# Moving the rows of a modulation product into the first mixer of a two-block transformer kernel

## The reference, cut to what matters

```python
def ada_mod(cond, w, b):
    m = jax.nn.silu(cond) @ w + b          # w: 1024 x 6144
    return jnp.split(m, N_MOD, axis=-1)
sh1, sc1, g1, sh2, sc2, g2 = ada_mod(c, w_ada, b_ada)              # for the tokens: all six used
csh1, csc1, ... = ada_mod(c_ctx, w_ada, b_ada)                     # for the context: two used
hx2 = modulate(rms_norm(x, norm2_g), sh2, sc2)                     # h * (1 + scale) + shift
x = x + g2 * sqrelu_mlp(hx2, w_mlp1, w_mlp2)
```

## Time and profile before

| | |
|---|---|
| median of 3 runs | 2599.49 us (2598.84 to 2599.61) |
| the profiled execution | 2597.69 us, its span 2595.9 us |
| PE busy | 2567.7 us, 99% |
| DVE, ACT, POOL busy | 1739.3 us (67%), 1172.8 us (45%), 206.0 us (8%) |
| DMA moved | 406.14 MB, mean 156 GB/s |
| PE's clock granted | 0.999 of full speed |

### The profile page before, as it was taken

The page is one execution under the profiler, slowest core; times in us unless marked ns, Lnnn a source line. Parts: engine busy times, 40 slices in busy tenths (PEclk is TensorE's granted clock), DMA queues, the critical chain, the costliest instruction groups (busy, mean ns, idle before and its releaser), DMA issues.

```text
span 2595.9 us, 41811 instructions
## 1 busy us (share of the span) xinstructions
PE 2567.7 (99%) x16880; PEld 2148.2 (83%) x16880; DVE 1739.3 (67%) x2471; ACT 1172.8 (45%) x1844; POOL 206.0 (8%) x245
## 2 busy tenths in 40 slices
PE   8999999999999999999999999999999999999999
PEld 7887878787888887887989878977887888888887
DVE  6454454559999978898725564566667777768573
ACT  6454444536444443356432343244545555554331
POOL 2121222300100001132000000000000000000000
PEclk9999999999999999999999999999999999999999
DMA  4101111235777799983423212121543444487763
GB/s 142 42 26 42 35 41 34 73 124 176 253 242 252 266 375 335 336 294 138 159 87 131 67 60 69 42 76 59 197 157 117 154 154 141 158 326 279 242 223 136
DMA packets 290769, 406.14 MB, mean 156 GB/s; under 512 B 15760, under 2 KB 162704, under 8 KB 290576
## 3 DMA queue, kind: packets, MB, share of 16 engines
q1 hardware_dynamic: 276464, 352.07, 39.7%
q0 software_dynamic: 14112, 51.39, 5.8%
HBM read 314.27 MB, written 89.13 MB: 155 GB/s over the span
## 4 chain that ended last, share of the span: by engine, by line
PE 70%; DVE 6%; DMA 3%; issue 2%; ACT 1%; SPq 0%; DVEq 0%; ACTq 0%
PE ps L973 14%; PE ps L903 7%; PE ps L905 7%; PE ps L901 7%; PE ps L579 3%; PE ps L563 3%; PE ps L566 3%; PE ps L689 3%; PE ps L1160 3%; PE ps L693 3%; PE ps L691 3%; PE ps L1161 2%; PE ps L1165 2%; PE ps L1135 1%; DVE mraw L2460 1%
## 5 line engine op out<-in xcount | busy, mean ns | idle before, releaser
L901 PE MATMUL ps<-Bh,Ah 128*128 128x512 f32 x896 | 349.6, 390 | 1.4 <-ACT vb L1715 1.4
L903 PE MATMUL ps<-Bh,Al 128*128 128x512 f32 x896 | 348.8, 389 | 1.5 <-DVE Al L2336 1.5
L2127 DVE TENSOR_TENSOR Wlo<-Wraw,Whi 128x1024 fp32r<-128x1024 f32 x100 | 124.6, 1262 | 217.5 <-ACT Whi L1533 217.4
L905 PE MATMUL ps<-Bl,Ah 128*128 128x512 f32 x640 | 249.0, 389 | 0.0
L1737 ACT ACTIVATE ftr_h<-ftr_r 128x1024 fp32r<-128x1024 f32 x112 | 118.6, 1059 | 237.6 <-DMA ftr_r<-b_scratch 237.4
L973 PE MATMUL ps<-ftr_l,wgt_h 128*128 128x512 f32 x848 | 210.1, 390 | 4.0 <-DVE ftr_l L2404 4.0
L689 PE MATMUL ps<-Whi,Hh 128*128 128x256 f32 x736 | 212.2, 288 | 0.0
L973 PE MATMUL ps<-ftr_h,wgt_h 128*128 128x512 f32 x848 | 210.0, 390 | 0.0
L973 PE MATMUL ps<-ftr_h,wgt_l 128*128 128x512 f32 x848 | 209.6, 389 | 0.0
L693 PE MATMUL ps<-Whi,Hl 128*128 128x256 f32 x736 | 208.2, 283 | 0.0
L691 PE MATMUL ps<-Wlo,Hh 128*128 128x256 f32 x736 | 208.2, 283 | 0.0
(11 more groups left out here) (383 smaller groups left out, 5463.6 us busy)
## 6 DMA issues: line engine op xcount, KB each, us to landing
b_scratch<-qb SPq DMA_DIRECT2D x224, 256.0 KB, 3.0
wgt_r<-in_m_w SPq DMA_DIRECT2D x112, 512.0 KB, 4.8
ftr_r<-b_scratch SPq DMA_DIRECT2D x112, 512.0 KB, 6.1
pair<-in_m_w SPq DMA_DIRECT2D x128, 256.0 KB, 3.2
mraw<-in_w_ada POOLq DMA_DIRECT2D x64, 512.0 KB, 4.6
Wraw<-in_w_in SPq DMA_DIRECT2D x56, 512.0 KB, 4.1
other<-in_m_w SPq DMA_DIRECT2D x32, 512.0 KB, 5.6
mraw<-in_m_w1T POOLq DMA_DIRECT2D x32, 512.0 KB, 5.1
```

What stands on the lines that cost most here:

```text
L901: e.matmul(o, h[:, k, :], Bh[x][:, k, :], start=first and k == 0, stop=False, skip_group_check=not first)
L903: e.matmul(o, l[:, k, :], Bh[x][:, k, :], start=False, stop=False, skip_group_check=not first)
L905: i = e.matmul(o, h[:, k, :], Bl[x][:, k, :], start=False, stop=k == 3, skip_group_check=not first)
L2127: e.tensor_tensor(Wlo[n % 4][:], Wraw[n % 2][:], Whi[n % 4][:].bitcast(F), ALU.subtract).then_inc(*S("w_lo", "v").tick(n))
```

## The change

Units 0 to 48 go into `MIX`: three after steps of head 0's g, six after steps of f for heads 1, 3 and 5, four after steps of q for heads 1 to 5, four after steps of g for heads 2 and 4. Units 49 to 65 go to the MLP's first stage at n = 8, 10, ... 40, the diagonal to n = 42, the shift row to product 44, units 66 to 97 to n = 46, 48, ... 108. The second stage has none left. The buffers of the tokens' rows are now two tiles of `R1` that the mixer has free (6 and 7, the vector in 5); ACT's copy into `R1` at tail 2 of heads 5 to 7 waits for unit 48, and SP's reload of x in the second stage for unit 97.

```diff
+            if (kind == "f" and h in (1, 3, 5) and i in (0, 1, 3, 4, 6, 7) or kind == "q" and 1 <= h < 6 and i in (0, 1, 4, 5)
+                    or kind == "g" and h in (2, 4) and i in (0, 1, 4, 5) or kind == "g" and h == 0 and i in (1, 4, 5)):
+                MIX.append(("mod", u, None))
+                u += 1
...
-        MODS = {}
-        for g in range(4, 53):
-            MODS[g] = [] if 8 <= g < 16 else list(range(49, NU))[sum(map(len, MODS.values())):][:2 if 18 <= g < 26 else 1]
+        DIAG, ROW = 42, 44
+        MODS = {**{8 + 2 * i: 49 + i for i in range(17)}, **{46 + 2 * i: 66 + i for i in range(32)}}
...
+                    if s == ROW and not j:
+                        shift_row()
...
-                            sp.wait_ge(S("ada").at(48))
+                            sp.wait_ge(S("ada").at(NU - 1))
...
+                        if h > 4:
+                            act.wait_ge(S("ada").at(48))
                         e.activation(R1[:, h, :], ps[:], ACT.Copy).then_inc(*freed(("tail", h, 2), 0))
...
+                elif kind == "mod":
+                    modulation(h)
...
+            def row_load(u):
+
+                if u % 49 >= 2:
+                    pool.wait_ge(S("ada").at(u - 2))
+                j = u - 1 if u < 49 else u - 50
+                e.dma_start(mod_place(u), w_ada[j] if u < 66 else m2_w1T[u - 66]).then_inc(*S("ada_raw", u % 2).tick(u, 16))
+
+            pool.wait_ge(sq_of(1).at((1, 7, 1, 0)), H1.lo_at(7))
+            vector_load(0)
...
+                if kind == "mod":
+                    if h < 48:
+                        row_load(h + 1)
```

More of the change, by code:

```diff
@@ L192, in build @@
         other = [at(f"other{i}", [P, 1024], F, WRA + 4096 * i) for i in range(2)]
-        cvec, shr = sa("cvec", 13), sa("shr", 12)
-        mraw = [[at(f"mraw{i}", [P, T], F, R1A + 22528 + 4096 * i) for i in range(2)], [sa("mraw2", 14), sa("mraw3", 15)]]
+        cvec, shr = [R1[:, 5, :], sa("cvec", 13)[:]], sa("shr", 13)
+        mraw = [[R1[:, 6 + i, :] for i in range(2)], [at(f"mraw{i}", [P, T], F, R1A + 22528 + 4096 * i)[:] for i in range(2)]]
         facc = [at(f"facc{a}", [P, T], F, H_(6 + a)) for a in range(2)]
@@ L321, in build @@
         MIX += [*in_turn(more, rest, 1), ("split", 7, None)]
+        mixed, MIX, u = MIX, [], 0
+        for step in mixed:
+            MIX.append(step)
+            kind, h, i = step
+            if (kind == "f" and h in (1, 3, 5) and i in (0, 1, 3, 4, 6, 7) or kind == "q" and 1 <= h < 6 and i in (0, 1, 4, 5)
+                    or kind == "g" and h in (2, 4) and i in (0, 1, 4, 5) or kind == "g" and h == 0 and i in (1, 4, 5)):
+                MIX.append(("mod", u, None))
+                u += 1
+        assert u == 49
         S = Sems()
@@ L906, in product, with shift_row @@
                 i.then_inc(*S("ps_full", b).tick(key))
+            def shift_row():
+                b, occ = PS["shift_row"] = 3, filled[3]
+                filled[3] += 1
+                empty(b, occ)
+                pe.wait_ge(S("shift_diag").at(0), S("const").at(0))
+                for cs in HALF:
+                    i = e.matmul(psum[b][:, cs], ones[:], shr[:, cs], start=True, stop=True)
+                full(i, b, occ)
             def mlp(j):
                 for s in range(NS * j, NS * j + NS):
+                    if s == ROW and not j:
+                        shift_row()
                     if s == NS * j + 2:
@@ L956, in stream @@
                     for g in range(8 * i, 8 * i + together):
[L957 to L963, removed]
                         if g == 51 and not j:
@@ L1583, in scalar_program, with vector_sigmoid @@
             rstd("norm1", 1, rstd1)
+            def vector_sigmoid(w, *place_free):
+                table(SIG)
+                act.wait_ge(S("c").at(w), *place_free)
+                e.activation(mod_place(49 * w), cvec[w], ACT.Sigmoid).then_inc(*S("c_sig").tick(w))
             for kind, h, i in MIX:
@@ L1588, in scalar_program @@
                     feed(upto(("f", h)))
+                elif kind == "mod" and h == 0:
+                    vector_sigmoid(0, H1.lo_at(6))
                 elif kind == "f_end":
@@ L1794, in first_stage @@
                         squared(s - 2)
-                    if j == 0 and n >= 8 and n % 2 == 0 and (n - 8) // 2 < 49:
-                        modulation((n - 8) // 2)
+                    if j == 0 and MODS.get(n) == 49:
+                        vector_sigmoid(1, S("xs_out").at(0), S("lo", "v").at(b_lo(0, 3, 3)))
+                    if j == 0 and n == ROW + 1:
+                        act.wait_ge(full_at("shift_row"))
+                        e.activation(shr[:], tile("shift_row")[:], ACT.Copy).then_inc(*freed("shift_row"))
                     if n in (NS - 3, NS - 2, NS, NS + 1):
@@ L1845, in scalar_program @@
                 step_split(0, g)
[L1846 to L1850, removed]
                 if g in FINAL_AT:
@@ L2189, in vector_program, with modulation @@
             feed(4)
+            def modulation(u):
+                raw, w = mod_place(u), int(u >= 49)
+                j = u - 1 - 49 * w
+                if j < 0:
+                    dve.wait_ge(S("c_sig").at(w))
+                    e.tensor_tensor(cvec[w], cvec[w], raw, ALU.mult).then_inc(*S("ada").tick(u))
+                    return
+                dve.wait_ge(S("ada_raw", u % 2).at(u))
+                if u < 66:
+                    dve.wait_ge(S("ada").at(49 * w))
+                    e.tensor_tensor_reduce(raw, raw, cvec[w], 1.0, vec[:, V_BADA + j:V_BADA + j + 1], ALU.mult, ALU.add,
+                                           mods[:, j, w:w + 1]).then_inc(*S("ada").tick(u))
+                else:
+                    dve.wait_ge(out_at("shift_row"))
+                    e.tensor_tensor_reduce(raw, raw, shr[:], 1.0, 0.0, ALU.mult, ALU.add,
+                                           shw[:, u - 66:u - 65]).then_inc(*S("ada").tick(u))
             for kind, h, i in MIX:
@@ L2471, in beside @@
             def beside(g):
[L2473 to L2479, removed]
                 if g in (49, 53):
@@ L2541, in first_stage @@
                         feature_sums(SEQ[s - 1][1] - 1)
-                    if j == 0 and n >= 8 and n % 2 == 0 and (n - 8) // 2 < 49:
-                        modulation((n - 8) // 2)
+                    if j == 0 and n in MODS:
+                        modulation(MODS[n])
+                    if j == 0 and n == DIAG:
+                        dve.wait_ge(S("ada").at(65), S("ident").at(0))
+                        for k in range(8):
+                            x = e.tensor_scalar(shr[:, 128 * k:128 * k + 128], ident[:], mods[:, 24 + k, 0:1], None, ALU.mult)
+                        x.then_inc(*S("shift_diag").tick(0))
                     if n in (NS - 2, NS - 1):
@@ L2841, in gpsimd_program, with vector_load @@
             e.memset(near[:], 0.0).then_inc(*S("acc_zero").tick(1))
+            def vector_load(w):
+                e.dma_start(cvec[w], c_d[w]).then_inc(*S("c").tick(w, 16))
+            def row_load(u):
[5 more added lines that the diff above has]
+            vector_load(0)
             for kind, h, i in MIX:
-                if kind == "level" and i:
+                if kind == "mod":
+                    if h < 48:
+                        row_load(h + 1)
+                elif kind == "level" and i:
                     lev, m = i, (1 << i) >> 1
@@ L2895, in final_add @@
                 e.tensor_tensor(to, to, ftmp[1][:], ALU.add).then_inc(*sum_of(5, 1).tick((5, n)))
-            for u in range(52):
-                modulation(u)
+            pool.wait_ge(full_at(("mlp_norm", 0), 1))
+            vector_load(1)
+            pool.wait_ge(S("xs_out").at(0), S("lo", "v").at(b_lo(0, 3, 3)))
+            for u in range(50, NU):
+                row_load(u)
             for g in range(4, 56):
-                for u in MODS.get(g, ()):
-                    if u >= 52:
-                        modulation(u)
                 if FINAL_AT.get(g, 11) not in (0, 4, 11):
```

39 lines of the change are left out of this document (removed).

## The result

The changed kernel takes 2631.77 us (median of 4 runs, 2629.32 to 2634.32), the kernel before on the same chip 2599.55 (2598.84 to 2601.23). The ratio is 1.0122, with a 95% interval of 1.0109 to 1.0134: slower by 1.2%. The forecast of 2623 has the right sign, and the range of 2609 to 2634 holds the time, but the size was 9 us short. The times are medians of executions at the normal clock; two executions, one of the kernel before (3118 us) and one of E3 (3860 us), ran at a lower clock throughout and are left out.

The account below looks back on a forecast made before the run. PE, busy 99% of the span, was taken as the bound, so only its waits matter. Terms 17.1 + 4.5 + 6.4 + 2.2 + 0 - 6.3 = +23.9 us on 2597.69 gave 2621.6, about 2623 as median; range 2609 to 2634.

Parts of the forecast that it names:

- B: q of heads 1 to 5: two rows delay the state's copy, costing PE's tail 2 0.9 us each; 4.5 us.
- Rivals 1 and 2: Rows' loads never delay DVE: 1, all rows hide, 2593, chance 0.08; 2, only tail 2's loss stays, 2597.7, chance 0.06.
- A: f of heads 1, 3 and 5, six rows each: f_end 5.7 us late, all PE's at tail 1; 17.1 us.
- C: g of heads 2 and 4, four rows each: PE waits 2.4 us at level 0's product, then 0.8; 6.4 us.
- D: g of head 0, three rows: level 0's product 1.4 us late, 0.8 more behind it; 2.2 us.
- E: MLP's first stage: 49 units as before, two more at its end; 0 us, ends -0.7 and +2.
- F: MLP's second stage: 49 row units and their loads go, so PE waits less for DVE's splits; -6.3 us.
- rival 3: MLP's second stage: its waits come from the DMA rate, not the rows, so no gain; 2629, chance 0.06.

Follow-up runs that it names:

- E3: The changed kernel with four row buffers instead of two for units 0 to 30 (heads 0 to 3): 2608.29 us, ratio 1.0032.
- E1: The changed kernel without the mixer's token row loads; DVE's row instructions stay in the same places: 2599.32 us, ratio 0.9997.
- E2: The changed kernel with its 49 row steps taken out of the mixer, no tokens' modulation computed: 2587.56 us, ratio 0.9953.
- E8: The kernel before with six extra DVE instructions ahead of f_end in heads 1, 3 and 5, no rows added: 2627.49 us, ratio 1.0104.
- E6: The changed kernel with POOL's level 1 step in heads 2 and 4 moved ahead of the row loads of g: 2627.59 us, ratio 1.0103.
- E10: The kernel before with all but the first two row loads of the MLP's second stage left out, DVE's instructions kept: 2588.21 us, ratio 0.9955.
- E9: The changed kernel's 49 units re-placed: behind levels 2 to 6, fewer in f and g, q rows behind the state's copy: 2587.96 us, ratio 0.9953.
- E11: The changed kernel with four row buffers for heads 0 to 3, run again for a profile: 2608.6 us, ratio 1.0037.
- E7: The kernel before with two extra DVE instructions ahead of f_end in heads 1, 3 and 5, no rows added: 2609.3 us, ratio 1.0034.

## Why the prediction was right, and where its size failed

The mechanism held: a row from the third of a group on waits for its landing, DVE holds what is behind it, and tail 1 has no spare time. E1 (no loads: of the 44 us by which the changed kernel is above E2 some 12 are left, B and the clock behind it), E3 (more buffers: 32 us of loss against the kernel before come down to some 9) and E8 (the lateness alone: 26.6 us) say so from three sides. Rivals 1 and 2, that the rows or most of them hide, fell with the waits on DMA. Term by term, on the profiled executions:

| term | forecast | measured | |
|---|---|---|---|
| A, f of heads 1, 3, 5 | 17.1 | 20.6 | `kST` 24.2 less 3.6 |
| B, tail 2 on `St` | 4.5 | 1.0 | heads 2 and 4, 0.5 each |
| C, g of heads 2, 4 | 6.4 | 9.9 | 5.3 + 4.6 |
| D, g of head 0 | 2.2 | 1.1 | waits of 0.45 and 0.56; shift 2.1 less the next line |
| start of the kernel | none | 1.0 | PE late before any row |
| slow clock, mixer | none | 11.1 | PE's busy time times what the clock lacks of 1.00, in windows of 5 us |
| E, first stage | 0 | -0.2 | +1.7, with 1.9 moved in from the second |
| F, second stage | -6.3 | -11.0 | -12.9 + 1.9 |
| later | 0 | +1.2 | 0.8 of it the wait on `Z`, 0.2 before |
| sum | 23.9 | 34.7 | span +34.4 |

**The step that failed is one that wasn't there.** "So the whole 5.7 us is PE's: 3 x 5.7" priced a stall at its length. Five stalls of 4.6 us or more took another 1.5 to 3.0 us each through the clock, 2.2 on average. E8 shows the same without any row. This is 11.1 us, more than the whole error. That the time still fell inside the range owes something to luck: the range had no term for the clock, and F and B came out 4.7 and 3.5 us lower than forecast.

**A** was short by 1.2 us a head. The landings, from issue to the row's start on DVE, were 5.3 and 3.8 us in head 1 against my 4.2, and the sixth row waited 0.47 more. The estimate that the prediction worked out from the Trainium skill ("DMA: Bandwidth & Descriptors", Anatomy of one DMA), 3.2 us, does not fit here: the median row between 60 and 470 us landed in 3.7.

**B** was forecast at 4.5, is 1.0 in the changed kernel and 9.1 in E1. In heads 2 and 4 tail 1 runs at full clock and PE waits as argued, but for 0.5 us and not 0.9 (two rows take 2.4 us, not 2.7):

```profile
159.54 0.46 PE L800 MATMUL ps<-q,St 128*128 128x128 f32 x2 [0.50 <-DVE St L2295]
```

In heads 1, 3 and 5, where tail 1 has stalled, PE runs it at the lower clock, so the state comes later against DVE and the two rows fit in front of it (DVE even waits 0.56 us for it in head 1). A and B are thus not to be added there: the bigger stall pays for the smaller. In E1 a row meets POOL's products, which "two rows take it to 97.8" left out. In the changed kernel these stand behind the loads and come later.

**C**: the landing was as forecast, the fourth row's duration was not: 3.88 us for 1.35. Of the 3.5 us that C is over, E6 gave back 3.1 (9.9 to 6.8 in heads 2 and 4). The prediction looked at POOL's product only as something PE waits for ("before DVE's own product is"), and not as something that runs beside a row.

**D**: DVE's product was done at 51.9, as forecast (52.0). PE was itself 1.0 us late from the kernel's start and so waited 0.45 us for it, not 1.4, then 0.56. That the shift of 2.1 us met the forecast of 2.2 is luck in its last part. **E** held.

**F** had the right effect under the wrong cause. "About 62 us of DVE, and their loads go" and rival 3 put DVE's time and the DMA rate against each other; E10 decides for the loads. By it the rows' time on DVE alone costs PE nothing there. Rival 3 read on from there that the gain would not be had. It was had in full, because those loads are the ones that moved away. The size, 11.0 instead of 6.3: all of the earlier trace rows and the rest of that stage's idle time, 6.9, and 1.7 of lower clock at 1200 to 1205 (granted 0.66). The cause of the last 2.4 us stays open.

## What to carry to other kernels

An instruction that waits for a transfer is priced by the transfer and by what stands behind it in its engine's queue, not by its busy time: with two buffers two of them are cheap, and the third costs a round trip. Ask of each place which engine's deadline is behind it, and put long waits where none is (E9: the same rows, the same 36 us of waiting on DVE, no loss). When a stall of the bounding engine is forecast, look in a trace at what its clock does after such stalls and give that a term of its own, and don't add the stalls of one chain without asking which one absorbs the next.

## What the runs showed of the hardware that I had not expected

- **The price of a stall on TensorE.** The ten stalls of 4.6 to 7.7 us in the changed kernel, E8 and E11 were all followed by matmuls at 1.2 GHz (3.31 to 3.33 us for the fourteen of tail 1 that take 1.80), at 1.5 to 3.0 us a stall. Shorter ones did not behave alike. Of E7's three stalls of 2.7 us one was followed by 1.7 us of it (2.78 us for the fourteen) and two by none. Those of 2.11 us in E1's head 4 and of 2.57 us in E6's head 2 were followed by 1.7 us each, and those of 1.61 and 1.42 us in E11 by none. In the kernel before, five short waits between 1194 and 1200 us, 2.8 us in sum, were followed by 1.7 us.
- **DVE beside POOL.** The rows' instruction reads two operands in SBUF and takes 1.28 us alone. It took 3.67 to 4.00 beside 2.5 us of POOL's two products (changed kernel and E6). The sum nearly holds: 1.28 + 2.5 = 3.8, as if the two took turns. In E1 POOL's first product began during a row. That row kept 1.28 us, the product took 2.49 instead of 1.50, and the next row, which began during the product, took 2.53. Which of the two engines bears the wait when they begin together the runs don't settle: at 182.4 it was DVE, in E1's first row POOL. The Trainium skill ("GPSIMD Engine Reference", Specifications) names the shared interfaces and a DVE instruction with two inputs in SBUF as a case of contention. The trace agrees, and adds the size.
